# A two-layer hybrid decoder step: the linear recurrence, the forget-gate logarithms and the gate silu move out of the linear-attention stage into the input projections

## The reference, cut to what matters

```
gq, gk, gv, gg, glr, lx, lgate, dq, dkv, kr = split((x * (1 + scale1) + shift1) @ w_in)
# group A, gated linear attention, 4 heads, key 32, value 64
logf = log_sigmoid(glr @ gla_w_gate + gla_b_gate) / 16
o, s_gla = gla(gq, gk, gv, logf, s0)            # chunks, a state carried from chunk to chunk
o_gla = rms_norm(o, gla_norm_g) * silu(gg)
# group B, RG-LRU, width 256
xc = causal_conv(lx, conv_buf, conv_w, conv_b)  # width 4
r, i = sigmoid(block_diag(xc, w_a) + b_a), sigmoid(block_diag(xc, w_x) + b_x)
a = exp(-8 * r * softplus(-lambda))
h[t] = a[t] * h[t-1] + sqrt(1 - a[t]**2) * (i * xc)[t]
o_lru = gelu(lgate) * h
```

## Time and profile before

| | |
|---|---|
| runs | 3541.36 (median), 3536.85 (lowest), 3542.70 (highest) us |
| span of the profiled execution | 3538.3 us |
| its own time outside the profile | not given apart from the three runs |
| PE busy | 3264.7 us, 92% of the span |
| DVE, ACT, POOL busy | 66%, 45%, 5% |
| HBM read, written | 306.41 MB, 6.51 MB |

### The profile page before, as it was taken

One profiled execution on the slowest core, in us unless ns is written; L12 is line 12 of the kernel. 1 busy time (PEld: TensorE's weight loads), 2 busy tenths in 40 slices (PEclk: granted clock), 3 DMA queues, 4 the chain that ended last, 5 costly groups with the idle time before them and its releaser, 6 DMA issues. The chain is left out here.

```text
span 3538.3 us, 61386 instructions
## 1 busy us (share of the span) xinstructions
PE 3264.7 (92%) x23676; PEld 2746.3 (78%) x23676; DVE 2324.4 (66%) x4406; ACT 1586.6 (45%) x3163; POOL 193.7 (5%) x252
## 2 busy tenths in 40 slices
PE   6988898998999998999989868989989999999997
PEld 4874556776898998999979535667769899899997
DVE  5136665444488889888842466644455888898878
ACT  5235454443354554444342545544442554544432
POOL 0011211110000000000000121111100000000000
PEclk9988899999999999999989969999989999999998
DMA  5035002442133332322111510034420333322231
GB/s 214 27 122 187 26 1 84 144 167 86 46 104 96 98 100 81 91 85 88 51 53 30 198 30 1 1 129 166 166 66 30 101 103 92 97 83 86 87 109 56
DMA packets 157572, 316.89 MB, mean 90 GB/s; under 512 B 18491, under 2 KB 85341, under 8 KB 146406
## 3 DMA queue, kind: packets, MB, share of 16 engines
q1 hardware_dynamic: 145766, 229.08, 20.7%
q0 software_dynamic: 11520, 83.89, 6.6%
HBM read 306.41 MB, written 6.51 MB: 88 GB/s over the span
## 5 line engine op out<-in xcount | busy, mean ns | idle before, releaser
L2392 ACT CAST w_ffn_hi<-w_ffn 128x512 fp32r<-128x512 f32 x616 | 371.1, 618 | 259.5 <-DVE w_ffn L2574 129.0
L444 PE MATMUL psum<-h_lo,w_ffn_hi 128*128 128x256 f32 (+1 forms) x1408 | 406.7, 289 | 0.0
L2586 DVE TENSOR_TENSOR w_ffn_lo<-w_ffn,w_ffn_hi 128x1024 fp32r<-128x1024 f32 (+1 forms) x366 | 383.6, 1048 | 12.5 <-ACT w_ffn_hi L2392 12.0
L443 PE MATMUL psum<-h_forms_hi,w_ffn_hi 128*128 128x288 f32 x1232 | 364.2, 296 | 3.4 <-DVE w_ffn_lo L2586 3.4
L445 PE MATMUL psum<-h_forms_hi,w_ffn_lo 128*128 128x288 f32 x1232 | 363.9, 295 | 0.0
L443 PE MATMUL psum<-h_hi,w_ffn_hi 128*128 128x256 f32 x1232 | 348.7, 283 | 11.4 <-DVE w_ffn_lo L2586 9.5
L443 PE MATMUL psum<-ffn_act_hi,w_down_hi 128*128 128x288 f32 (+1 forms) x992 | 332.4, 335 | 21.5 <-DVE w_down_lo L2592 6.8
L445 PE MATMUL psum<-h_hi,w_ffn_lo 128*128 128x256 f32 x1232 | 346.8, 282 | 0.0
L445 PE MATMUL psum<-ffn_act_hi,w_down_lo 128*128 128x288 f32 (+1 forms) x992 | 326.7, 329 | 0.0
L444 PE MATMUL psum<-ffn_act_lo,w_down_hi 128*128 128x288 f32 (+1 forms) x992 | 325.9, 329 | 0.0
L429 DVE SCALAR_TENSOR_TENSOR xT<-psum,adaT,xT 128x512 f32<-128x512 f32 (+2 forms) x320 | 191.4, 610 | 129.9 <-PE psum L445 126.7
(11 more groups left out here) (452 smaller groups left out, 7631.0 us busy)
## 6 DMA issues: line engine op xcount, KB each, us to landing
w_ffn<-in_w_gu SPq DMA_DIRECT2D x352, 256.0 KB, 2.6
w_ada_pair<-in_w_ada SPq DMA_DIRECT2D x40, 1024.0 KB, 5.2
w_down<-in_w_down SPq DMA_DIRECT2D x192, 192.0 KB, 2.4
w_ada_first<-in_w_ada SPq DMA_DIRECT2D x4, 2048.0 KB, 23.0
w_out<-in_w_out SPq DMA_DIRECT2D x16, 512.0 KB, 7.2
w_in_T<-in_w_in_T SPq DMA_DIRECT2D x12, 512.0 KB, 4.4
w_down<-in_w_down SPq DMA_DIRECT2D x48, 128.0 KB, 2.1
z<-in_x_prompt SPq DMA_DIRECT2D x8, 512.0 KB, 7.3
```

Of the source, the lines that this page charges most:

```text
L443: pe.matmul(o, wh, xh, start=first, stop=False)
L444: pe.matmul(o, wh, xl, start=False, stop=False)
L2392: act.copy(WGH[:, (j + 1) % NR].bitcast(F32R), WGR[:, m % 2, i]).then_inc(s_wh, 1)
L2586: dve.tensor_tensor(WGL[:, m % 2, i:i + n].bitcast(F32R), WGR[:, m % 2, i:i + n], WGH[:, r:r + n], ALU.subtract).then_inc(s_wl, n)
```

## The change

1. At the start of `stage_in` SP stores XT (128 rows of 8704 words, 4.46 MB) to a buffer in device memory, `residual_kept`, and waits for it. It is loaded again in `stage_mla_prompt`, behind that stage's other DMAs. In between, the space of XT holds the arrays of the recurrence, two more buffers for `w_ada`, and the block-diagonal sample states.
2. The work list of `stage_in` grows by three G items (the nine transposes), three W items (the gate product) and twelve L items (the RG-LRU gates). The T outputs come in the order lx, lx, gq, gk, lgate, lgate. ACT, DVE and POOL get the logarithms, the silu of gg with its norm weights, the convolution, the sigmoids, the recurrence and the scans, at given places of the list. The gelu is applied as lgate is read from PSUM.
3. `stage_gla` begins with `cumulate(0)` and `cumulate(1)`, which have a PSUM bank each, so that `cumulate(s+1)` stands one step ahead. The sample block comes fifth (`SEQ`), its states have a buffer of their own, and its last products go to two row groups. The copy of the attention output moves from DVE to ACT. The chunk decay is read from the exponentials instead of by an Exp of its own. The tail is in three parts, of which two stand within the loop. `pair` is spread 1, 2, 3, 3, 3, 3, 3, 3, 2, 1 over the steps (first layer) or 1, 2, 2, 2, 2, 2, 2, 2, 1, 0 (second), with four load buffers.

```diff
+        XKEPT = nc.dram_tensor("residual_kept", (P, KD * T), F32, kind="Internal").ap()
...
-        WAN = at("w_ada_pair", o_ht + 4 * T * 4, [P, 2, 2, KD, P])
+        NWA = 4
+        WAN = [at(f"w_ada_pair_{i}", o, [P, 2, KD, P]) for i, o in enumerate(
+            (o_ht + 4 * T * 4, o_ht + 4 * T * 4 + 8 * KD * P, o_xt + 2 * T * 4, o_xt + 2 * T * 4 + 8 * KD * P))]
...
-            items = [("B", b, 0) for b in range(NBLK)] + [("A", b, 0) for b in range(NBLK)]
-            items += [("T", m, n) for m in range(NT) for n in range(3)]
+            items = [("B", b, 0) for b in range(NBLK)] + [("A", b, 0) for b in range(2)]
+            items += [("G", x, 0) for x in range(3)] + [("A", b, 0) for b in range(2, 5)]
+            items += [("W", x, 0) for x in range(3)] + [("A", b, 0) for b in range(5, NBLK)]
+            for j in range(NT):
+                items += [("T", j, n) for n in range(3)]
+                if j in (1, 2):
+                    items += [("L", j - 1, k) for k in range(6)]
...
+                    sp.dma_start(XKEPT, XT.rearrange("p k t -> p (k t)")).then_inc(s_xs, 16)
+                    sp.wait_ge(s_xs, 16)
...
+                        if (kind, i) == ("A", 2):
+                            latent_squares()
+                        if (kind, i) == ("A", 5):
+                            log_gates()
+                        if (kind, i, n) == ("T", 0, 0):
+                            silu()
+                        if (kind, i, n) == ("T", 3, 0):
+                            recurrence()
+                        if (kind, i, n) == ("T", 3, 2):
+                            root()
...
+        ADA_PER_STEP = {24: (1, 2, 3, 3, 3, 3, 3, 3, 2, 1), 16: (1, 2, 2, 2, 2, 2, 2, 2, 1, 0)}
+        SEQ = (0, 1, 2, 3, SMP, 4, 5, 6, 7)
+        SQUARES_AT, RMS_AT, GATED_AT = (7, 9), (8, 9), (9, 10)
...
+                    for c in range(2):
+                        pool.tensor_tensor(HT[:, 2 + c], LG[:, c], XC[:, c], ALU.mult).then_inc(s_mx, 1)
+                    pool.wait_ge(s_mx, 2)
+                    pool.memset(SBS, 0.0).then_inc(s_z, 1)
...
+                    cumulate(0)
                     pe.wait_ge(s_az, 1)
-                    pair(0)
-                    pe.wait_ge(s_ab, len(GCHUNKS))
-                    cumulate(0)
-                    pe.wait_ge(s_li, 48)
-                    pair(1)
-                    pair(2)
-                    for c in range(2):
-                        for w in range(2):
-                            lru_gates(c, w)
-                            pair(3 + 2 * c + w)
+                    cumulate(1)
                     for s in range(1, NBLK + 2):
+                        todo = list(pairs_of(s - 1))
                         if s <= NBLK:
+                            if s + 1 < NBLK:
+                                cumulate(s + 1)
+                            for q in todo[:1]:
+                                pair(q)
                             attend(s - 1)
+                        for q in todo[1:2]:
+                            pair(q)
                         if s >= 2:
                             output(s - 2)
+                        for q in todo[2:] if s <= NBLK else todo:
+                            pair(q)
...
+                    sp.dma_start(XT.rearrange("p k t -> p (k t)"), XKEPT).then_inc(s_xb, 16)
                     sp.wait_ge(s_out, 64)
+                    sp.wait_ge(s_xb, 16)
```

More of the change, by code:

```diff
@@ new lines, in root, with gelu @@
+                    def root():
+                        for c in range(2):
+                            act.wait_ge(s_lf, c + 1)
+                            act.activation(LR[:, c], LR[:, c], ACT.Sqrt).then_inc(s_lq, 1)
+                    def gelu(g, i, n):
+                        t0, w = GROUPS[n]
+                        act.wait_ge(s_mn, 1)
+                        act.wait_ge(s_mm, g + 1)
+                        act.activation(LG[:, TSEQ[i] - 4, t0:t0 + w], bank(g % 8)[:, 0:w],
+                                       ACT.Gelu_apprx_tanh).then_inc(s_ev[0], 1)
@@ new lines, in keep, with rms @@
+                    def keep(p):
+                        blk = SEQ[p]
+                        n = rows(blk)
+                        act.wait_ge(s_o, p + 1)
+                        if blk == SMP:
+                            act.wait_ge(s_z, 1)
+                        act.copy(OG[0:n, blk, :], bank(3)[0:n, 0:256]).then_inc(s_oc, 1)
+                    def rms(i):
+                        b0, b1 = PARTS[i]
+                        v = GS[:, H_GLA * b0:H_GLA * b1]
+                        act.wait_ge(s_n, i + 1)
+                        act.activation(v, v, ACT.Sqrt, scale=1.0 / DV, bias=EPS[:, 1:2]).then_inc(s_sq, 1)
```

923 lines of the change are left out of this document (477 added, 446 removed).

## The result

| | before | changed |
|---|---|---|
| median of the runs shown with the result | 3539.34 us | 3481.33 us |
| lowest, highest | 3536.85, 3542.70 | 3475.69, 3488.44 |
| ratio, with its 95% interval | | 0.9837 (0.9824 to 0.985) |
| span of the profiled execution | 3538.3 us | 3483.5 us |

The changed kernel is faster by 1.6%, 58 us by the medians and 54.8 us by the two traced spans. A second set of five runs of it, beside the experiments, gave 3477.85 us and a ratio of 0.9835 (0.9809 to 0.9862).

A forecast was written before the change was run, and what follows sets the result against it. PE was taken to bound `stage_in` and nearly fill the loop of `stage_gla`. Gains of 39.6 and 46.4 us less 24 in `stage_in` gave 62: span 3476, median 3479, range 3452 to 3508.

The forecast's parts named there:

- steps 3 to 8: Loop of `stage_gla`: 59 us in the first layer (9.3 a step plus 3), 48 in the second (7.5 plus 3).
- the start: `stage_gla` until step 2 ends: 24 us, from 12 PE work, 5 waits, 4 half clock, 3 POOL against DVE.
- the tail: End of `stage_gla`, steps 9 and 10 and the last part: 19 us, 20 with the barrier.
- `stage_in`, PE's moved work: Transposes, gate product and RG-LRU gates moved into `stage_in` cost PE their full length: 12 us per layer.
- margin of 2.7 us: `stage_in`: DVE's last split ends at about 21.8 us, PE needs it at 24.5; any excess makes PE wait.
- recurrence late in `stage_in`: ACT and DVE miss the margin by some 5 us, or POOL holds the convolution: 10 us, 3489; chance 0.10.
- The residual: The 4.46 MB store at the start of `stage_in` takes 11 to 36 us within 71 us of room: costs nothing.
- slower by the store: A slow store makes PE wait before the first W item: at 35 GB/s 56 us per layer, 3591; chance 0.04.
- A sign of being wrong: In the loop of `stage_gla`: the prediction is wrong if the three-pair step is over 10.5 us.
- bound by latency: The loop's circle between engines outlasts PE's work, 11 and 9.3 us a step: 21 us, 3500; chance 0.09.
- More is gained: `stage_gla`: start 17 us, steps 8.8, tail 15, so 15 us less per layer, 3450 to 3460; chance 0.12.
- Does nothing: PE's moved work and new waits eat what the head of `stage_gla` gave: 3535 to 3541; chance 0.03.

The follow-up runs named there:

- e4: The changed kernel with each of the twelve RG-LRU gate items of `stage_in` multiplied twice on PE; 3494.2 us, ratio 0.9884.
- e5: The changed kernel with ACT repeating the recurrence's Ln pass three more times over both halves in `stage_in`; 3494.2 us, ratio 0.9863.
- e3: The changed kernel with the residual stored five times in a row instead of once, POOL waiting for the fifth; 3477.6 us, ratio 0.9836.
- e1: The changed kernel with POOL's two `HT` products in `stage_gla` started only after the states of steps 1 and 2; 3465.5 us, ratio 0.9785.
- e10: The changed kernel with the edits of e1 and e2 together, plus fewer spare PE products than e9; 3444.9 us, ratio 0.9738.
- e2: The changed kernel with ACT's copy of the second pair's rows put ahead of `blocks_of(s-1)` instead of behind it; 3470.3 us, ratio 0.9794.
- e9: The changed kernel with spare PE products: 40 behind `cumulate(1)`, 5 ahead of the second pair in steps 2, 3 and 4; 3472.3 us, ratio 0.9822.
- e13: e10 with `cumulate(s)` at the start of step s, as in the kernel before, instead of `cumulate(s+1)`; 3448.9 us, ratio 0.9738.
- e6: The changed kernel with the sample block last in `SEQ`, as in the kernel before; 3472.2 us, ratio 0.9809.
- e14: e10 with two load buffers for `w_ada` instead of four; 3469.6 us, ratio 0.9806.

## Why the prediction came out right

3479 was forecast, and 3481.3 and 3477.9 were measured, inside the range. The mechanism is the one forecast, but that the median fits to 2 us is in part luck. The span was to be 3476 and was 3483.5: steps 3 to 8 took 13.9 us more than forecast in the two layers, and the start, the tail and the other stages 7.1 us less. The terms, against the traced run:

| term | forecast | measured, layer 1 and 2 |
|---|---|---|
| `stage_in`, PE's moved work | +12 | +12.2, +12.3 |
| start of `stage_gla` to the end of step 2 | 24 | 21.9, 22.1 |
| steps 3 to 8 | 59 and 48 | 64.4, 56.5 |
| tail | 20 | 19.2, 19.2 |
| the other stages | 0 | -1.5 for both |
| gain in the span | 62 | 54.8 |

- **`stage_in`.** The moved PE work cost its length, and the gates ran at the full clock; e4 shows that it is the bound. ACT's root ended 19.7 us behind the start of output four (19.5 forecast), DVE's split at 21.9 (21.8), and PE wanted it at 24.1 (24.5). The margin of 2.7 us was 2.2, and e5 shows that it was really that close: what is put on top comes out as a wait of PE. The rival "recurrence late in `stage_in`" was 2.2 us away.
- **The residual.** The cost of nothing was right. The store took 19.2 us of the 71, within the bounds of 11 and 36; e3 puts the rival "slower by the store" far off. The load back (14.2 us) cost nothing either: the other stages took 1.5 us less than before.
- **The start.** The parts of the 24 were off in opposite directions. Work was 12.3 us at full clock where 12 was taken (the prediction counts three `cumulate` where there are four, and 1.9 us for an `attend` that takes 1.6). The half clock covered 7 us, but PE was busy for only 3.2 of them, which is 1.6 us of loss and not 4. PE idled for 8.0 us, as forecast (5 + 3), but 4.4 of them are POOL's and 3.6 the other waits. The Trainium skill, page SBUF — State Buffer, section Who interferes with whom, has the two engines shut each other out for the whole of an instruction; the trace agrees here, DVE's 5.56 us being POOL's 4.95 and little more, and e1 removes 4.4 of them. Both products stood in the way, as the prediction worked out by that rule, but they took 2.5 us each and not 3.2.
- **Steps 3 to 8**, the term that was mis-sized: "9.3" and "7.5" us a step plus 3. At the full clock the steps were 8.5 to 9.4 and 6.9 to 7.9 us, no worse than forecast; the third pair waited 0.59 us, as said (0.5), but only in three of the six steps. But I gave the half clock 4 us, all of it at the start, and wrote that PE is nearly full in the loop. PE was full, and still granted half its clock for 17 us in the first layer and 26 in the second, which is 8 and 13 us of loss. e10 gets it back, e2 and e9 in one layer each. The excess of 5.4 and 8.5 us over the forecast is less than this loss, so nothing else is needed to explain it.
- **A sign of being wrong did show.** The prediction called itself wrong if the three-pair step is over 10.5 us, and steps 3 and 4 took 14.7 and 11.9. The mean step, without the 3 us for the sample block, was 10.2 and 8.9 us, somewhat nearer to the rival "bound by latency" (11 and 9.3) than to the forecast (9.3 and 7.5). The length alone could not have told the two apart; the granted clock does, and e13.
- **The tail** was right, and ended on DVE's normalization as the prediction had it.
- **The rivals.** "Bound by latency" falls with e13. "More is gained" (a start of 17 us, clock soon back) is what e10 makes of it, by 3 small edits: its step 2 ends 17.0 us into the stage in both layers. "Does nothing" never stood.

Where the gain came from: the head and the gates, 36 us of each stage before, are gone, PE's share of them paid back with 12 us in the stage ahead, where it runs at the full clock. The tail went from 34.6 to 19 us. The loop has taken the pairs that the head and the gates had covered. No run puts one of these parts back as it was, so this split of the gain rests on the traces of the two kernels.

## What to carry to other kernels

Work of ACT and DVE that is moved under a stage in which TensorE is the bound is free down to the last microsecond of a chain that can be added up from rows; TensorE's own work is not, so move it only where it runs at a better clock than at its old place. In a short stage of small products, count a wait of TensorE twice: once for its length, and once for the half clock that may follow and outlast it many times over. Compare such kernels by the lengths of their stages and the granted clock in them before a median is believed: four different edits here all had lower medians than the kernel they started from, the intervals of three of them overlap its own, and one of them (e6) owes its shorter stage to the clock alone.

## What was not expected of the hardware

- TensorE's granted clock stood at half (1.2 of 2.4 GHz) for 17 to 37 us at a stretch while TensorE was busy for 92% of it or more (e14: 34.17 of 37.30 us busy at a mean clock of 0.53). Ahead of such falls stood waits of 0.9 to 1.5 us within steps; the same waits were followed by a fall in some executions and layers and not in others (e2: not in the first layer, but in the second). What decides this is open.
- With spare products in the waits the clock stayed up at the start of the stage in 9 of 10 cases, and without them in none of 16 (e10: 4 and 8 us at half clock, in the tail, against 30 and 45; part of that may belong to its shorter waits).
- A store of 4.46 MB with 34.8 KB in a partition ran at 371 GB/s when alone, three times the rate of the one store of 256 KB that the trace before shows (125 GB/s), and TensorE waited for nothing in that time.
